# V rows gathered as 32 tokens by 4 experts per transfer, and summed with 128x32 weights

## What is computed

```python
qh = (xb @ wq).reshape(PEER_BLOCK, PEER_HEADS, 2, PEER_HALF)
s1 = jnp.einsum('thd,nd->thn', qh[:, :, 0], keys1).astype(jnp.float32)
s2 = jnp.einsum('thd,nd->thn', qh[:, :, 1], keys2).astype(jnp.float32)
v1, i1 = lax.top_k(s1, PEER_TOPK)
v2, i2 = lax.top_k(s2, PEER_TOPK)
cand = (v1[..., :, None] + v2[..., None, :]).reshape(PEER_BLOCK, PEER_HEADS, PEER_TOPK * PEER_TOPK)
sc, ci = lax.top_k(cand, PEER_TOPK)
e = (jnp.take_along_axis(i1, ci // PEER_TOPK, axis=-1) * PEER_KEYS
     + jnp.take_along_axis(i2, ci % PEER_TOPK, axis=-1))
gate = jax.nn.softmax(sc, axis=-1)
act = jax.nn.gelu(jnp.einsum('td,thkd->thk', xb, u_tab[e]).astype(jnp.float32)) * gate
return jnp.einsum('thk,thkd->td', act.astype(xb.dtype), v_tab[e])
```

## Time and profile before

| | |
|---|---|
| median of 3 runs | 3465.75 us |
| profiled execution: span from the first to the last instruction | 3605.3 us |
| share of the span: PE, DVE, POOL, ACT | 84%, 65%, 64%, 18% |
| share of the span in which the 16 DMA engines move the gathered rows | 83.1% |
| bytes moved | 1213.76 MB, of which 1107.43 MB are U and V rows |
| granted TensorE clock, mean | 0.959 |

### The profile page before, as it was taken

One profiled execution on the slowest core, in us unless ns is written; L12 is line 12 of the kernel. 1 busy time (PEld: TensorE's weight loads), 2 busy tenths in 40 slices (PEclk: granted clock), 3 DMA queues, 4 the chain that ended last, 5 costly groups with the idle time before them and its releaser, 6 DMA issues.

```text
span 3605.3 us, 39214 instructions
## 1 busy us (share of the span) xinstructions
PE 3011.3 (84%) x10724; PEld 1568.6 (44%) x10724; DVE 2354.0 (65%) x5813; ACT 658.5 (18%) x2015; POOL 2298.7 (64%) x2132
## 2 busy tenths in 40 slices
PE   7687888889987898879987798879987799877677
PEld 2553454345533454345533454345533454344222
DVE  3565975578656875578756876568655876568442
ACT  2211221112211221112211221112211121111111
POOL 0224666766777566766676567667676567667775
PEclk9799999989999999999999999999998999999999
DMA  6456989999999999999999999999999999999998
GB/s 241 161 174 240 366 316 346 371 354 351 337 372 378 348 338 351 348 361 359 330 368 357 363 314 355 361 340 369 341 353 355 364 327 345 350 375 373 355 368 296
DMA packets 340167, 1213.76 MB, mean 337 GB/s; under 512 B 41072, under 2 KB 41200, under 8 KB 339904
## 3 DMA queue, kind: packets, MB, share of 16 engines
q0 software_dynamic: 304128, 1107.43, 83.1%
q1 hardware_dynamic: 35776, 103.32, 7.7%
HBM read 1205.73 MB, written 4.87 MB: 336 GB/s over the span
## 4 chain that ended last, share of the span: by engine, by line
PE 37%; issue 20%; DMA 16%; DVE 9%; POOL 9%; another core or an unknown queue 6%; ACT 3%; POOLq 0%; ACTq 0%; SPq 0%; DVEq 0%
PE acc L428 23%; PE bank L428 13%; DMA ring<-peer_v,idx 11%; POOL ring L404 9%; DMA ring<-peer_u,idx 6%; DVE ring L1266 2%; ACT xn L750 1%; ACT diag L750 1%; DVE kw L1050 1%; DVE xn L1161 0%; DVE xn L1164 0%; ACT h L750 0%; ACT xT L750 0%; DVE topi L1052 0%
## 5 line engine op out<-in xcount | busy, mean ns | idle before, releaser
L428 PE MATMUL acc<-ring,diag 128*128 128x512 f32 (+1 forms) x4224 | 2086.7, 623 | 449.9 <-DMA ring<-peer_v,idx 269.1
L1266 DVE SCALAR_TENSOR_TENSOR ring<-ring,xcur 128x1024 f32<-128x1024 f32 x1056 | 1289.0, 1225 | 818.0 <-DMA ring<-peer_u,idx 744.5
L404 POOL DMA_INDIRECT ring<-peer_v,idx x1056 | 1151.2, 1090 | 643.6 <-issue 291.9
L404 POOL DMA_INDIRECT ring<-peer_u,idx x1056 | 1143.7, 1083 | 642.7 <-issue 316.5
L428 PEld LDWEIGHTS acc<-ring,diag 128*128 128x128 f32 (+1 forms) x4224 | 746.4, 192 | 1427.7 <-issue 1107.3
L750 ACT ACTIVATE diag<-ident,coef 128x128 f32<-128x128 f32 x1024 | 366.7, 395 | 646.7 <-PE acc L428 392.6
L428 PEld LDWEIGHTS bank<-xT,win 128*128 128x128 f32 (+1 forms) x2304 | 272.9, 183 | 79.2 <-issue 73.5
L428 PE MATMUL bank<-xT,win 128*128 128x128 f32 (+1 forms) x2304 | 282.6, 277 | 2.4 <-ACT xT L750 2.4
L750 ACT ACTIVATE G<-bank 128x128 f32<-128x128 f32 (+1 forms) x137 | 40.6, 296 | 830.4 <-PE bank L428 449.4
L428 PE MATMUL bank<-win,xT 128*128 128x512 f32 (+3 forms) x368 | 166.2, 583 | 1.9 <-ACT xT L750 1.9
L428 PEld LDWEIGHTS bank<-xT,qk 128*128 128x128 f32 x1024 | 131.5, 201 | 37.1 <-issue 37.1
(11 more groups left out here) (227 smaller groups left out, 1821.1 us busy)
## 6 DMA issues: line engine op xcount, KB each, us to landing
qk<-wq SPq DMA_DIRECT2D x64, 512.0 KB
t<-wq SPq DMA_DIRECT2D x64, 512.0 KB
ring<-peer_u,idx POOLq DMA_INDIRECT x1056
ring<-peer_v,idx POOLq DMA_INDIRECT x1056
win<-w_in SPq DMA_DIRECT2D x6, 2048.0 KB, 15.1
ring<-wq SPq DMA_DIRECT2D x16, 512.0 KB, 5.1
wout<-w_out SPq DMA_DIRECT2D x1, 4096.0 KB, 22.8
xn<-x_prompt SPq DMA_DIRECT2D x8, 512.0 KB
```

What stands on the lines that cost most here:

```text
L404: pool.indirect_dma_start(out=ring[:, slot, :], out_offset=None, in_=(peer_u, peer_v)[which], in_offset=bass.IndirectOffsetOnAxis(ap=idx[: ...
L428: return nc.tensor.matmul(out, lhsT, rhs, start=start, stop=stop)
L1266: stt(row, row, 1.0, xcur[:, :], ALU.mult, ALU.mult, accum_out=dots[:, column(b, e):column(b, e) + 1]).then_inc(s_dot, 1)
```

## The change

The V rows are gathered in another layout. Before, transfer j brought expert j of all 128 tokens, token p on partition p. Now transfer j brings four experts of one group of 32 tokens (group j % 4): partition 32q + t holds the row of token 32 (j % 4) + t and the q-th of the four experts. The sum needs then only a 128x32 matrix (`wv`: the 32-column pattern `rep` scaled by a coefficient for each partition), and its output goes to the 32 partitions of `acc` of that group. Four transfers in a row write four different groups of output partitions. What it brings with it:

- Indices and coefficients must be laid out anew, token and expert together on the partitions, for each head. PE does it with four small matmuls with selecting matrices `takes` (`spread_choice` from `ef`, `spread_coef` from `coef`), DVE copies the indices out in four pieces (`idxv`), ACT the coefficients (`coefv`).
- V runs 18 ticks behind U, not 16 (LAG), with 8 `wv` buffers for 4 `diag`.
- The mixer has four banks for six, with other waits for a bank that is still in use.
- A head's two score matrices lie in one bank, for every head the same one, so the scores of a head wait for the sorts of the head ahead.
- Of the sample stream (32 tokens) the V rows keep their layout.

The core of the diff. Of the two functions named `spread_choice` the first is PE's and the second DVE's; `query` is shown for PE and then for DVE, `spread_coef` for ACT.

```diff
+SETS = 8
+LAG = TOPK + 2
+GROUPS = P // SAMPLE
...
+                    if which == V and b is not None and e % TOPK == 0:
+                        pool.wait_ge(s_idxv, b * PEER_HEADS + e // TOPK + 1)
...
+                    rows_at = idx[:, column(b, e):column(b, e) + 1]
+                    if which == V and b is not None:
+                        rows_at = idxv[:, group_column(e):group_column(e) + 1]
...
             def expert_sum(b, j):
...
-                pe.wait_ge(s_diag, experts_before(b) + j + 1)
+                pe.wait_ge(s_wv, experts_before(b) + j + 1)
+                lo = 0 if b is None else SAMPLE * (j % GROUPS)
+                final = j == n - 1 if b is None else j >= n - GROUPS
                 for half in range(2):
-                    last = mm(acc[0:n, 512 * half:512 * half + 512], diag[:, j % DIAGS, 0:n],
+                    last = mm(acc[lo:lo + SAMPLE, 512 * half:512 * half + 512], wv[:, j % SETS, :],
                               ring[:, slot, 512 * half:512 * half + 512], start=False, stop=final)
...
+            def spread_rows(out, values, done):
+
+                for g in range(GROUPS):
+                    last = mm(spread_of(out)[:, g, :], takes[:, g, :], values)
+                last.then_inc(done, 1)
...
+            def spread_choice(b, head, tick):
...
+                pe.wait_ge(s_sel, heads_before(b) + head + 1)
...
+                spread_rows(bB, ef[:, :], s_idx_ps)
...
-                    if half == 0 and head >= 2:
-                        pe.wait_ge(s_topk, heads_before(b) + head - 1)
+                    if half == 0 and head >= 1:
+                        pe.wait_ge(s_topk, heads_before(b) + head)
                     pe.wait_ge(s_q2, b * 16 + ft + 1)
-                    mm(bank[2 * (head % 2) + half][:, 0:P], q2[:, half, :], keysT[:, half, :]).then_inc(s_score, 1)
+                    mm(bA[:, P * half:P * half + P], q2[:, half, :], keysT[:, half, :]).then_inc(s_score, 1)
...
+            def spread_coef(b, g, tick):
+
+                act.wait_ge(s_coef_ps, b * PEER_HEADS + g + 1)
+                act.wait_ge(s_wv, experts_before(b))
+                for q in range(COPIES):
+                    mine = slice(SAMPLE * q, SAMPLE * q + SAMPLE)
+                    last = a(coefv[mine, TOPK * g:TOPK * g + TOPK].rearrange("p (g k) -> p g k", g=GROUPS),
+                             spread_of(spread_bank(tick))[mine, :, GROUPS * q:GROUPS * q + GROUPS], ACT.Copy)
+                last.then_inc(s_coefv, 1)
...
-                a(diag[:, j % DIAGS, 0:n_experts(b)], rep[:, :] if b is None else ident[:, :], ACT.Copy,
-                  scale=coef[:, column(b, j):column(b, j) + 1]).then_inc(s_diag, 1)
+                a(wv[:, j % SETS, :], rep[:, :], ACT.Copy, scale=at).then_inc(s_wv, 1)
...
             def query(b, head, step, tick):
...
-                if step < 2:
-                    dve.wait_ge(s_score, b * 16 + 2 * head + 1 + step)
+                if step == 0:
+                    dve.wait_ge(s_score, b * 16 + 2 * head + 2)
...
+            def spread_choice(b, head):
+
+                dve.wait_ge(s_idx_ps, b * PEER_HEADS + head + 1)
+                for q in range(COPIES):
+                    mine = slice(SAMPLE * q, SAMPLE * q + SAMPLE)
+                    last = dve.tensor_copy(idxv[mine, TOPK * head:TOPK * head + TOPK].rearrange("p (g k) -> p g k", g=GROUPS),
+                                           spread_of(bB)[mine, :, GROUPS * q:GROUPS * q + GROUPS])
+                last.then_inc(s_idxv, 1)
```

More of the change, by code:

```diff
@@ L453, in project_part, with mixer @@
                     return last
-            def mixer(v, w, n, full, tick):
+            def mixer(v, w, n, full, tick, b=None):
                 if tick == T_XT:
@@ L698, in beside @@
                     query(b, head, tick - T_QUERY - QUERY_TICKS * (head - 1))
+                head = picked_head(tick)
+                if head is not None:
+                    spread_choice(b, head, tick)
+                if tick % TOPK == 1 and tick > TOPK:
+                    spread_coef(b, tick // TOPK - 1, tick, more)
                 if more:
-                    mixer(b + 3, b + 2, P, True, tick)
+                    mixer(b + 3, b + 2, P, True, tick, b)
                     query(b + 1, 0, tick - T_QUERY0)
+                    if tick == T_QUERY0 + 9:
+                        spread_choice(b + 1, 0, tick)
             for tick in range(T_MIXER, BLOCK_TICKS):
@@ L714, in _ @@
                     query(0, 0, t - T_QUERY0)
-            for tick in range(TOPK):
-                expert_sum(None, SAMPLE - TOPK + tick)
+                    if t == T_QUERY0 + 9:
+                        spread_choice(0, 0, t)
+            for tick in range(LAG):
+                expert_sum(None, SAMPLE - LAG + tick)
                 beside(0, tick, False)
@@ L893, in query @@
                         act.wait_ge(s_score, b * 16 + ft - 1)
[L894 removed]
+                    a(q2[:, half, :], bank[2 + half][:, 0:P], ACT.Copy).then_inc(s_q2, 1)
                 if step == 7:
@@ L959, in _ @@
             take_over(None)
+            for g in range(GROUPS):
+                last = a(takes[:, g, :].rearrange("p (q t) -> p q t", q=COPIES),
+                         spread(ident[:, SAMPLE * g:SAMPLE * g + SAMPLE].unsqueeze(1), 1, COPIES), ACT.Copy)
+            last.then_inc(s_takes, 1)
             for tick in range(T_MIXER, BLOCK_TICKS):
@@ L972, in _ @@
             gelu_exp(None, 1)
-            for tick in range(TOPK):
-                diagonal(None, SAMPLE - TOPK + tick)
+            for tick in range(LAG):
+                weights(None, SAMPLE - LAG + tick)
+                if tick == TOPK:
+                    gelu_exp(0, 0)
                 beside(0, tick, False)
@@ L991, in _ @@
             b = BLOCKS - 1
-            for tick in range(TOPK, BLOCK_TICKS + TOPK):
+            for tick in range(LAG, BLOCK_TICKS):
                 if tick % TOPK == 0:
                     gelu_exp(b, tick // TOPK - 1)
-                diagonal(b, tick - TOPK)
-                if tick < BLOCK_TICKS:
-                    beside(b, tick, False)
+                weights(b, tick - LAG)
+                beside(b, tick, False)
+            for tick in range(LAG):
+                if tick == 0:
+                    gelu_exp(b, PEER_HEADS - 1)
+                weights(b, P - LAG + tick)
+                if tick == 1:
+                    spread_coef(b, PEER_HEADS - 1, tick)
             finish(b)
@@ L1301, in beside @@
                     query(b, head, tick - T_QUERY - QUERY_TICKS * (head - 1), tick)
+                head = picked_head(tick)
+                if head is not None:
+                    spread_choice(b, head)
                 if more:
@@ L1329, in _ @@
                     query(0, 0, t - T_QUERY0, t)
-            for tick in range(TOPK):
+                    if t == T_QUERY0 + 9:
+                        spread_choice(0, 0)
+            for tick in range(LAG):
+                if tick == TOPK:
+                    coefficients(0, 0)
                 dots_of(0, tick)
@@ L1337, in _ @@
                 restart()
-                for tick in range(TOPK, BLOCK_TICKS):
+                for tick in range(LAG, BLOCK_TICKS):
                     if tick % TOPK == 0:
@@ L1342, in _ @@
                     beside(b, tick, True)
-                for tick in range(TOPK):
+                for tick in range(LAG):
                     if tick == 0:
                         coefficients(b, PEER_HEADS - 1)
+                    if tick == TOPK:
+                        coefficients(b + 1, 0)
                     dots_of(b + 1, tick)
```

271 lines of the change are left out of this document (175 added, 96 removed).

## The result

The changed kernel takes 3603.39 us (median of four runs, 3592.84 to 3618.26), the kernel before on the same chip 3465.29 us: 1.041 of it, 95% interval 1.037 to 1.045. It is slower by 138 us, where I had predicted 50 us less.

The account below looks back on a forecast made before the run. No engine was full; POOL, which every transfer passes, was taken as the clock, with DMA 0.95 busy. -90 + 37 + 10 - 8 - 2 = -53 us (-1.5%) gave 3415 us, range 3345 to 3520 us.

Parts of the forecast that it names:

- C, ACT: ACT's weight matrices and coefficient copies: 312 ns for 395 a matrix, 85 us less work, ACT 18% busy, so no gain.
- A, PE relief: Expert sums on PE: neighbours overlap, 1.3 us saved each, up to 42 us a block; -90 us, ends 0 and -164.
- My first rival: PE's sums don't overlap where it counts, or column-width changes cost PE: +42 us, 3506 us, chance 17%.
- the rival in which the transfers are the limit: POOL's slot waits go but issue grows as much, DMA 0.95 busy: sum -3 us, 3463 us, chance 18%.
- the 299 us of waits: POOL's waits in the first profile: 225.5 us for PE and 73.9 us unnamed; 60%, 180 us, expected to go.
- B and the new wait: DVE's index conversion and copies, +37 us (0 to +46), and its wait for PE's small matmuls, +10 us (0 to +140).
- D: The loop's end, PE's wait behind `take_up`: coefficients made two ticks earlier, -1 us a block, -8 us, ends 0 and -24.
- E: The kernel's end: last 16 sums overlap, -6 us, against two more V transfers and later coefficients; -2 us, ends -8 and +5.
- Banks: Six banks become four, so PE waits for readers that were free before; these are 16 us and more ahead: nothing.
- the neighbours' closer starts: Sign of being right, on PE: neighbouring sums start closer than 1.7 us.
- the last sums under 1.5 us each: Sign of being right, at the kernel's end: the last 16 sums take under 1.5 us each.
- POOL's waits for PE: Sign of being right, on POOL: its waits for PE fall well below 225 us.

Follow-up runs that it names:

- e5: Changed kernel without the relayout of indices (V gathered by the old `idx`), the coefficients' half kept: 3577.02 us, 1.0331 of the kernel before.
- e1: Changed kernel without any relayout of indices and coefficients; 128x32 weights and four groups of output partitions kept: 3463.46 us, 1.0004 of the kernel before.
- e11: Changed kernel with V 20 experts behind U and ACT copying the coefficients a tick later, behind the next tick's matrix: 3542.25 us, 1.0238 of the kernel before.
- e9: Changed kernel with PE's takes matmuls of the coefficients ahead of their tick's sum, not behind it: 3525.73 us, 1.0171 of the kernel before.
- e2: Changed kernel without relayout and with 128x128 diagonals again; four banks, one score bank and 18 ticks stay: 3465.56 us, 1.0006 of the kernel before.
- e0: The kernel before, unedited, profiled a second time: 3465.32 us, profile span 3463.3 us.
- e6: Changed kernel without the relayout of coefficients (weights take the old `coef`), the indices' half kept: 3503.84 us, 1.0119 of the kernel before.
- e7: Changed kernel with DVE copying the indices out one tick after PE's matmuls, nothing left out: 3591.78 us, 1.0363 of the kernel before.
- e3: Changed kernel with a fifth bank, which takes the scores of odd heads: 3603.87 us, 1.0433 of the kernel before.
- e8: Changed kernel with V 20 experts behind U instead of 18, nothing left out: 3605.83 us, 1.0422 of the kernel before.

## Why the prediction was wrong, by its steps

- **C, ACT, nothing: the larger of the two steps that failed.** I wrote that its four copies "come once a head, a tick ahead of their use", and took nothing. They are a tick ahead for the head's own coefficients, but the matrix of the next tick stands behind them on ACT, and ACT's wait for PE ahead of both. Alone this half costs 113 us (e5 against e1), and a change of order alone takes back 64 to 78 us (e11, e9). I had asked for DVE's wait what is queued behind it, and not for ACT's, since ACT was 18% busy. Busy share says nothing of that.
- **A, PE relief, -90: nothing, the other step that failed.** Neighbours do run beside each other (a pair saves 0.44 us at one place and 1.39 at the best, with the change of width in it, for my 1.3), but I had put the change of the column width at nothing, because the trace didn't show it, and it costs about as much as the neighbours gain: 111 us for 121 by busy time (e1 against e2). Rows 6 could hardly show it. They begin with the sum, and 0.19 of the 0.31 us lie ahead of it. My first rival had this very mechanism, at up to 0.19 us twice and 32 us a block, and A at nothing; without the relayout's terms its sum gives 3461 us, and e1, the change without its relayout, takes 3463.46. That this is also the 3463 us of the rival in which the transfers are the limit is luck, as that sum holds 47 us for a relayout that e1 doesn't have. Besides, the 299 us of waits that A was to shorten are 168 us in e0.
- **B and the new wait, +37 and +10: right.** e6 against e1 is 40 us. I had B at 0.66 us a head; at the one place shown the five ticks are 1.12 us longer; the wait is 25.8 us in all and e7 finds 12 us or less.
- **D, -8: right at its place.** From PE's last matmul ahead of `take_up` to the first sum behind it are 10.2 us in e0 and 9.3 in the changed kernel (means of six turns of the loop), about the 1 us forecast, by another road. The wait behind `take_up` falls by more, from 5.7 to 2.5 us, and the wait ahead of it and `take_up` itself give back most of it. At the end of one turn PE idles 3.02 us before `take_up` and 3.00 us behind it, for 2.26 and 5.04 in the earlier trace rows, and the four passes of `take_up` take 3.61 us for 1.98 (3.51 in e1):

```profile
1190.98 0.96 PE L458 MATMUL bank<-coef,takes 128*128 128x16 f32 x8
1194.97 3.61 PE L458 MATMUL acc<-h,ident 128*128 128x512 f32 x4 [3.02 <-ACT xn L852]
1201.58 3.23 PE L458 MATMUL acc<-ring,wv 128*32 128x512 f32 x4 [3.00 <-ACT wv L852]
```

  Here the copies of head 0's coefficients stand ahead of the copy of `acc` that `take_up` waits for.
- **E, -2: too small to tell.** The last 19 sums are 8 us shorter in e1 than in e2, with no shorter span.
- **Banks: nothing, right** (e2, e3).

As measured: 0 for A, 40 for the indices, 113 for the coefficients, less 13 that the two share, 140 us.

Of the signs that I named for being right, the neighbours' closer starts and the last sums under 1.5 us each came true; POOL's waits for PE did not, with 220.5 us for "well below 225". The neighbours did what they should, and PE as a whole had no less to do.

The part of the clock is only an estimate. The mean granted clock is 0.965 in the changed kernel and 0.975 in e9. Below full speed are (1 - 0.965) x 3602 = 126 us and (1 - 0.975) x 3529 = 88 us, so some 38 us of PE's time, beside the 72 us of idle time. No run here took the one without the other.

## What to carry to other kernels

Before a hand-over goes through a third engine (PE to ACT to PE), list what stands behind the wait in that engine's program, above all what the waiting partner needs next; more distance for the data doesn't help if the order stays (e8), a later place for the consumer's copy does (e11), and so does an earlier place for the producer (e9). Set a saving against what its neighbours in the program pay for it: here the sums took 121 us less and cost PE 111 us around them. And compare the profile's own time with the median before building a sum on its waits.

## What the runs showed of the hardware that I had not expected

- The width change: 0.31 us for a sum of 128x32 weights between projections with 128 columns in their weights (3.75 for 3.43 us with one of them), while two neighbours on different 32-column groups with nothing to wait for ran side by side, 1.92 us for the two, and longer sequences came at 1.03 to 1.35 us each. The end of the changed kernel, where 32 passes are 8 sums and 24 passes 6:

```profile
3573.73 8.25 PE L458 MATMUL acc<-ring,wv 128*32 128x512 f32 x32 [1.27 <-ACT wv L852]
...
3586.63 8.12 PE L458 MATMUL acc<-ring,wv 128*32 128x512 f32 x24 [0.60 <-DMA ring<-peer_v,idxv]
```

- Behind PE's wait of 2.35 us, amid dense work, the granted clock was 0.50, in the changed kernel and in e8 (2.97 and 2.76 us for a sum). Behind e9's wait of 0.53 us it was 1.00 (1.90 us). A short wait of PE for another engine can so cost its length and a part of it again, here 2.35 us and 1.07.
